# A decoder trunk on one core: compression tiles moved into the recurrence's fill, group norm products spread over projection tiles, three fill chunks per attention step

## The chip, the core and the metric

The kernel runs on one core of a Trainium2 chip. The metric is the device time in microseconds (us) of one execution, the median of several. Below, PE is TensorE, DVE is VectorE, ACT is ScalarE, POOL is GpSimd, SP is the queue that issues most transfers.

## The reference

One decoder layer over 512 tokens of width 1024, all in float32. What matters here:

```python
h = rms_norm(x, norm_pre_mix[l])
proj = h @ w_in[l]
p_rwkv, p_nsa, p_swa, p_gate = _split(proj, (RWKV_COLS, NSA_COLS, SWA_COLS, GATE_COLS))
o_rwkv = rwkv7_time_mix(p_rwkv, ...)   # recurrence over time, then group norm, bonus, output gate g
o_nsa = nsa_mix(p_nsa, ...)            # k_cmp = compress(kc, ..), v_cmp = compress(vc, ..), softmax branches
o_swa = swa_sink_mix(p_swa, ...)       # window of 128 keys with a sink
gates = jax.nn.sigmoid(p_gate)
merged = gates[0] * (o_rwkv @ w_branch[0]) + gates[1] * (o_nsa @ w_branch[1]) + gates[2] * (o_swa @ w_branch[2])
x = x + rms_norm(merged @ w_out, norm_post_mix)
# then a SwiGLU FFN with norms, residual
```

`compress` takes the keys (or values) of NSA in 31 overlapping blocks of 32 tokens, adds a position table `pe`, multiplies the 2048-long blocks by `w1` (2048x256), applies gelu and multiplies by `w2`.

## The kernel before, in words

**Jobs.** Every dense product is a job of the list `JOBS`: one 128-column tile of a weight matrix, 8 chunks of 128 rows (`cmp`: 4 chunks of 128 rows by 256 columns). Order: 14 `rwkv`, 11 `nsa`, 6 `swa`, 5 `gate`, 8 `cmp` (4 for the keys, 4 for the values), 19 more `gate`, then branches, output, FFN. SP loads each tile into one of four buffers `WRAW`. It is split in a high part `WHI` (a rounded copy, by ACT or, for the jobs in `POOL_HI`, by POOL, L568) and a low part `WLO` (always POOL, L564; 128x256 pieces at L599 in attention). There are two split buffers: tile n can be converted when tile n-2 is done, and PE waits at a tile's first chunk for `w_lo`, that is for the whole tile. A chunk is three matmuls (L1481 to L1483; L1489 to L1491 for `cmp`, whose moving operand is the weights and whose stationary operand is the gathered, split input `XHI`, `XLO`). PE accumulates tiles in two banks `DB` by turns (`cmp` in `R[5]`), and DVE evacuates (L999, L1010); a tile starts when the last but one is evacuated. `swa` and `gate` tiles up to a point (`SPILLED`) go through two stage buffers `SQ` to DRAM.

**Fill.** While PE works on the recurrence, the group norm and attention, whose small products depend on DVE and ACT, it calls `fill(point)` between them, which does `FILL[point]` chunks of the next jobs. DVE calls `evacs(point)` at the matching places. The last fill of the gate tiles is `PT_SPLIT`, ahead of the branches.

**Recurrence** (`PT_CP`, four double chunks of time `cp`): in each, five doubling levels `lv`. A level is `pairs(R[0])`, a fill, the wait for `UI` (DVE, L1179), `pairs(R[1])` and `pairs(R[2])`, a fill. Fills of one chunk stand between the levels, larger ones around them (6 at the second point of a `cp`, 4 at its end, 2 at its start).

**Group norm** (`PT_GN`): mean products, variance products, the broadcast of 1/std from 8 rows, the gate product, and four bonus products `gn_bonus(m)`, each of which writes `R[4]` and must wait until DVE has read the one before. Before it DVE gathers `XF` (L1231, 8 operations for keys, 8 for values), copies `XHI` and subtracts to `XLO` (L1234, L1235) for `cmp`. Fills here: 3, 46, 16, 16 (the `cmp` tiles), 8, 16. Then transposes, gelu's second layer, and attention.

**Attention** (`PT_ATT`, 52 steps: for each of four query blocks `i` one compressed step and eight of NSA, keys 128 to 512, then sixteen sliding window steps `swa`): at step n PE does the scores product `qk(n)` (L1764), the fill, the transposes of step n-2 (L1525), the product with the values of step n-3 (L1811). DVE: scores(n), then the reciprocal of step n-1 (L1333). POOL at step n: the weights of step n-1 (`weigh`, L623, L625), then `split_upto(FILLED[PT_ATT + n] + 8)`, which converts pieces of two chunks until 8 chunks past the end of fill n. `FILLED` is the running sum of `FILL`.

```python
            for n in range(NST + 3):
                ...
                if 1 <= n < NST + 1:
                    weigh(n - 1)
                split_upto(int(FILLED[PT_ATT + n]) + 8)
```

Of the kernel before, what the change touches and what calls it, by code (L numbers as in the profile page):

```python
# [24 lines left out]
F32 = mybir.dt.float32  # L25
# [80 lines left out]
for _n in range(11):  # L106
    JOBS.append(("nsa", _n, 0, 8))
SW0 = len(JOBS)
# [3 lines left out]
NGA = 5  # L112
_gates = [("gate", _i, 0, 8) for _i in list(range(3 * GS, 3 * KC)) + list(range(3 * GS))]
JOBS += _gates[:NGA]
CMP0 = len(JOBS)

for _n in range(8):
    JOBS.append(("cmp", _n // 4, _n % 4, 4))
CMP1 = len(JOBS)
NGG = 3  # L120
JOBS += _gates[NGA:3 * (KC - GS)]
# [21 lines left out]
POOL_HI = [n for n in range(NS0, MERGE0) if not CMP0 <= n < CMP1 + NGG]  # L143
# [25 lines left out]
def group_of(n):  # L169

    return sum(not is_cmp(m) for m in range(n))
# [31 lines left out]
PT_ATT = len(FILL); FILL += [2] * (NSA_STEPS + 3)  # L203
# [3 lines left out]
FILL += [2 * (_rest // (2 * (NST - NSA_STEPS)))] * (NST - NSA_STEPS)  # L207
# [30 lines left out]
def build(nc, x, w_in, w_branch, w_out, w_gate, w_up, w_down, w2, a2, g2, ck1, ck2, cv1, cv2, sinks, rel_bias,  # L238
# [49 lines left out]
    T1 = at("T1", 98, [P, 2, 4, C])  # L288
# [21 lines left out]
    XHI = at("XHI", 90, [P, 2, 16, 2 * NCMP], F32R)  # L310
    XLO = at("XLO", 98, [P, 2, 16, 2 * NCMP], F32R)
    XF = at("XF", 52, [P, 16, 2 * NCMP])
# [7 lines left out]
    HG = at("HG", 70, [2 * NCMP, 2, CH])  # L320
# [65 lines left out]
    def split_of(n):  # L386
# [30 lines left out]
    xsplit_ok, cmp_read, hg_u, hg_t, hg_ok, kv_mm, kv_ok = (sem(s) for s in (  # L417
        "xsplit_ok", "cmp_read", "hg_u", "hg_t", "hg_ok", "kv_mm", "kv_ok"))
# [79 lines left out]
    with block:  # L498
# [161 lines left out]
        def _(act):  # L660
# [7 lines left out]
            def hi_part(n):  # L668

                act.wait_ge(w_loaded[n % NRAW], loaded_value(n))  # L670
                if n >= NSPL:
                    act.wait_ge(dense_done, slot_free(n))
                if n in (CMP0, MERGE0):
# [56 lines left out]

            act.wait_ge(cum_ok, 4)
            chunk_exps(0)
            for cp in range(4):
# [9 lines left out]
                for lv in range(1, 6):  # L743
# [7 lines left out]
                    if lv == 4:  # L751
                        act.wait_ge(bkt_T, cp + 1)
                        for c in range(2):
                            act.activation(BKT[:, c, :, :], R[4 + c][:, :].rearrange("p (m n) -> p m n", m=4),
                                           ACT.Copy).then_inc(bkt_ok, 1)
                for c in range(2):
# [14 lines left out]
            hi_part(CMP0)  # L771
            hi_part(CMP0 + 1)
# [4 lines left out]
            act.wait_ge(xsplit_ok, 2)  # L777
            for kv, w in enumerate((ck2, cv2)):
                act.dma_start(CW2[:, kv, :, :], w.rearrange("(h p) d -> p h d", p=P)).then_inc(cw2_in, 16)
            for n in range(CMP0 + 2, CMP0 + 6):  # L780
                hi_part(n)

            def hidden_tanh(kv):
                act.wait_ge(hg_u, kv + 1)
                act.activation(HT[:, kv, :], HT[:, kv, :], ACT.Tanh, scale=0.7978845608028654).then_inc(hg_t, 1)

            act.wait_ge(gn_var, 1)
            act.activation(SSUM[0:NH, :], R[0][0:NH, :], ACT.Sqrt, scale=1.0 / HD, bias=EPSC[0:NH, 1:2]).then_inc(gn_std, 1)
# [14 lines left out]
            act.wait_ge(dense_evac, group_of(NS0 + 10) + 1)  # L803
# [187 lines left out]
        def _(dve):  # L991
# [9 lines left out]
            def evac(n):  # L1001
# [16 lines left out]
                elif kind == "cmp":  # L1018
                    if part == 3:
                        gelu(n, i)  # L1020
                    return
                ins.then_inc(dense_evac, 1)

            def gelu(n, kv):

                dve.wait_ge(dense_done, n + 1)
                dve.tensor_copy(HG[:, kv, :], R[5][0:2 * NCMP, 0:CH]).then_inc(cmp_read, 1)
                dve.wait_ge(cmp_read, kv + 1)
                link(dve.tensor_tensor(HT[:, kv, :], HG[:, kv, :], HG[:, kv, :], ALU.mult))
                link(dve.tensor_scalar(HT[:, kv, :], HT[:, kv, :], 0.044715, 1.0, ALU.mult, ALU.add))  # L1030
                dve.tensor_tensor(HT[:, kv, :], HT[:, kv, :], HG[:, kv, :], ALU.mult).then_inc(hg_u, 1)
                dve.wait_ge(hg_t, kv + 1)
                link(dve.scalar_tensor_tensor(out=HG[:, kv, :], in0=HT[:, kv, :], scalar=1.0, in1=HG[:, kv, :],
                                              op0=ALU.add, op1=ALU.mult))
                dve.tensor_scalar(HG[:, kv, :], HG[:, kv, :], 0.5, None, ALU.mult).then_inc(hg_ok, 1)

            def evacs(point):

                while NS0 + state["evac"] < DONE[point]:
                    n = NS0 + state["evac"]  # L1040
                    if n == CMP0:
                        chain.settle()
# [90 lines left out]

            scaled_bk(0)
            for cp in range(4):
# [39 lines left out]
                for lv in range(1, 6):  # L1175
# [9 lines left out]
                    if lv == 2:  # L1185
# [4 lines left out]
                                          PCS.unsqueeze(2).broadcast_to([P, NH, P]), ALU.mult).then_inc(bkend_ok, 1)  # L1190
                    evacs(pt + 2 + 2 * (lv - 1))
                    evacs(pt + 3 + 2 * (lv - 1))
                for c in range(2):
# [11 lines left out]
                    if c == 0 and cp < 3:  # L1205
# [4 lines left out]
                                      R[2][:, 0:256].rearrange("p (a b) -> p a b", a=4), ALU.add).then_inc(st_ok, 1)  # L1210
                evacs(pt + 16)
# [6 lines left out]

            dve.wait_ge(y_ok, 8)
            for kv in range(2):  # L1220
                dve.wait_ge(dense_evac, group_of(NS0 + 10) + 1)
                pe = PARC[:, PAR["pe"] + 32 * kv:PAR["pe"] + 32 * kv + 32]
                for l in range(2):
                    for g in range(2):
                        p = slice(64 * g, 64 * g + 64)

# [748 lines left out]
```

## Time and profile before

| | us |
|---|---|
| median of 3 runs | 1158.3 (1156.88 to 1160.41) |
| the profiled execution | 1164.61 |
| its span | 1162.7 |
| recurrence, 138.4 to 346.1 | 207.7 |
| group norm and compression, 346.1 to 455.4 | 109.3 |
| attention with its last fills, 455.4 to 659.9 | 204.5 |
| branches, output, FFN, from 659.9 | 502.8 |

PE is busy for 94% of the span. Times of stages are on the profile's clock, from the span's start; "PEclk" in the rows is TensorE's granted clock as a share of full speed.

### The profile page before, as it was taken

The page shows a single profiled execution, that of the slowest core. Times are in us where ns is not written, and L with a number is a line of the kernel's source. Part 1 is how long each engine was busy: PE and PEld are TensorE (multiplying, and loading weights), DVE is VectorE, ACT ScalarE, POOL GpSimd, SP SyncE. Part 2 cuts the span into 40 slices and gives each one's busy share as a digit, 9 for nine tenths or more (in the row PEclk, how much of TensorE's full clock was granted, in tenths as well). Part 3 has the DMA queues.
Part 4 walks back from the last instruction along what each step waited for, and adds up shares of the span by engine and source line. Part 5 has one row for each costly group of instructions (what it writes and reads, how often), then busy time and mean ns, then how long its engine had stood idle before and what let it go on. Part 6 is the DMA issues. An engine that isn't in the chain of part 4 may idle for free.

```text
span 1162.7 us, 19062 instructions
## 1 busy us (share of the span) xinstructions
PE 1087.3 (94%) x7608; PEld 846.5 (73%) x7608; DVE 549.1 (47%) x910; ACT 357.5 (31%) x675; POOL 501.8 (43%) x431
## 2 busy tenths in 40 slices
PE   5998899989996899999998899999999999999996
PEld 3775577777775657666676677788888888888885
DVE  5786744463647162445444367234454454431113
ACT  4222212212110242444444344453322322322222
POOL 1444222221322644665578544743444444444442
PEclk9998899999998989999999999999999999999998
DMA  7343111100233524422111253732333333223231
GB/s 208 91 106 76 46 38 38 39 20 2 80 91 96 186 73 119 136 56 58 34 37 28 72 181 112 234 90 62 100 92 98 100 91 100 83 83 92 86 99 72
DMA packets 166046, 101.83 MB, mean 88 GB/s; under 512 B 21013, under 2 KB 154399, under 8 KB 165976
## 3 DMA queue, kind: packets, MB, share of 16 engines
q1 hardware_dynamic: 162336, 95.96, 28.7%
q10 hardware_dynamic: 3608, 4.88, 1.7%
q8 instruction: 51, 0.84, 0.3%
q14 instruction: 19, 0.16, 0.0%
q0 software_dynamic: 32, 0.00, 0.0%
HBM read 93.19 MB, written 7.63 MB: 87 GB/s over the span
## 4 chain that ended last, share of the span: by engine, by line
PE 80%; DVE 10%; POOL 4%; issue 2%; ACT 2%; DMA 1%; DVEq 0%; ACTq 0%; SPq 0%; POOLq 0%
PE ps L1481 20%; PE ps L1483 18%; PE ps L1482 18%; PE ps L1612 5%; PE ps L1525 3%; PE ps L1764 2%; PE ps L1811 2%; POOL WLO L564 2%; DVE XF L1231 1%; PE ps L1834 1%; PE ps L1836 1%; PE ps L1835 1%; DVE MT L1379 1%; POOL EB L625 1%; DMA PRAW<-in_par 1%
## 5 line engine op out<-in xcount | busy, mean ns | idle before, releaser
L564 POOL TENSOR_TENSOR WLO<-WRAW,WHI 128x1024 fp32r<-128x1024 f32 (+3 forms) x150 | 316.9, 2114 | 346.9 <-ACT WHI L926 197.0
L1481 PE MATMUL ps<-HHI,WHI 128*128 128x512 f32 x776 | 321.7, 415 | 18.1 <-DVE SQ L999 9.6
L1482 PE MATMUL ps<-HLO,WHI 128*128 128x512 f32 x776 | 305.9, 394 | 0.0
L1483 PE MATMUL ps<-HHI,WLO 128*128 128x512 f32 x776 | 305.9, 394 | 0.0
L1481 PEld LDWEIGHTS ps<-HHI,WHI 128*128 128x128 f32 x776 | 147.4, 190 | 75.5 <-issue 29.3
L1483 PEld LDWEIGHTS ps<-HHI,WLO 128*128 128x128 f32 x776 | 147.7, 190 | 32.3
L1482 PEld LDWEIGHTS ps<-HLO,WHI 128*128 128x128 f32 x776 | 147.9, 191 | 27.1 <-issue 1.0
L568 POOL CAST WHI<-WRAW 128x256 fp32r<-128x256 f32 (+1 forms) x83 | 49.0, 590 | 209.5 <-PE ps L1483 209.5
L926 ACT ACTIVATE WHI<-WRAW 128x1024 fp32r<-128x1024 f32 (+2 forms) x72 | 67.5, 937 | 140.0 <-PE ps L1483 140.0
L675 ACT ACTIVATE WHI<-WRAW 128x1024 fp32r<-128x1024 f32 (+1 forms) x55 | 47.8, 870 | 151.1 <-PE ps L1483 134.2
L1432 DVE TENSOR_TENSOR FT<-FT 128x512 f32<-128x512 f32 x22 | 50.9, 2313 | 89.0 <-ACT FT L932 89.0
L825 ACT ACTIVATE EB<-EB,MISC 128x257 f32<-128x257 f32 (+5 forms) x96 | 50.7, 530 | 73.5 <-DVE MISC L1319 59.6
L1481 PE MATMUL ps<-DHI,WHI 128*128 128x512 f32 x176 | 70.0, 398 | 0.2
L1483 PE MATMUL ps<-DHI,WLO 128*128 128x512 f32 x176 | 68.6, 390 | 0.0
L1482 PE MATMUL ps<-DLO,WHI 128*128 128x512 f32 x176 | 68.6, 390 | 0.0
L1449 DVE TENSOR_TENSOR SSUM<-SSUM,SQ 128x512 f32<-128x512 f32 x8 | 14.4, 1794 | 105.1 <-ACT SQ L964 105.1
L623 POOL TENSOR_SCALAR EB<-EB,MISC,GLT 128x128 f32<-128x128 f32 (+3 forms) x64 | 38.3, 607 | 42.1 <-DVE MISC L1333 42.0
L1339 DVE COPY PTB<-ps 128x256 f32<-128x256 f32 (+3 forms) x52 | 23.1, 445 | 60.4 <-PE ps L1525 60.3
L599 POOL TENSOR_TENSOR WLO<-WRAW,WHI 128x256 fp32r<-128x256 f32 x60 | 43.8, 730 | 5.0
L1481 PE MATMUL ps<-OHI,WHI 128*128 128x512 f32 x96 | 38.9, 405 | 5.4 <-POOL WLO L564 5.4
L1319 DVE CUSTOM_DVE_ANT_0 EB<-ps,TB 128x128 f32<-128x128 f32 (+3 forms) x64 | 28.9, 489 | 28.1 <-PE ps L1764 27.8
L934 ACT ACTIVATE DHI<-FT 128x512 f32 (+1 forms) x22 | 13.9, 632 | 88.4 <-DVE FT L1437 88.4
(295 smaller groups left out, 1655.8 us busy)
## 6 DMA issues: line engine op xcount, KB each, us to landing
WRAW<-in_w_in SPq DMA_DIRECT2D x47, 512.0 KB, 4.0
WRAW<-in_w_gate SPq DMA_DIRECT2D x22, 512.0 KB, 3.9
WRAW<-in_w_up SPq DMA_DIRECT2D x22, 512.0 KB, 3.9
WRAW<-in_w_down SPq DMA_DIRECT2D x16, 384.0 KB, 3.5
spilled<-SQ SPq DMA_DIRECT2D x21, 256.0 KB, 2.3
WRAW<-in_w_down SPq DMA_DIRECT2D x16, 320.0 KB, 3.1
WRAW<-in_w_in SPq DMA_DIRECT2D x16, 256.0 KB, 3.5
WRAW<-in_w_branch SPq DMA_DIRECT2D x32, 128.0 KB, 2.8
```

Source lines behind the costliest of these rows:

```text
L564: return pool.tensor_tensor(lo[:, 0:chunks, :], WRAW[:, n % NRAW, 0:chunks, :], hi[:, 0:chunks, :].bitcast(F32), ALU.subtract)
L568: return pool.tensor_copy(WHI[:, n % NSPL, k0:k1, :], WRAW[:, n % NRAW, k0:k1, :])
L599: lo = pool.tensor_tensor(WLO[:, n % NSPL, k:k + 2, :], WRAW[:, n % NRAW, k:k + 2, :], WHI[:, n % NSPL, k:k + 2, :].bitcast(F32), ALU.subt ...
L623: last = pool.tensor_scalar(e, e, rd, GLT[:, i, at0:at0 + 1], ALU.mult, ALU.mult)
L675: act.activation(split_of(n)[0][:, 0:width_of(n), :], WRAW[:, n % NRAW, 0:width_of(n), :], ACT.Copy).then_inc(w_hi, 1)
L825: last = act.activation(EB[:, n % 3, g, 0:w], EB[:, n % 3, g, 0:w], ACT.Exp, scale=-1.0, bias=st[:, g:g + 1], accum_out=st[:, 2 + g:3 + g])
L926: act.activation(WHI[:, n % NSPL, 0:chunks, :], WRAW[:, n % NRAW, 0:chunks, :], ACT.Copy).then_inc(w_hi, 1)
L1432: dve.tensor_tensor(FT[:, b + 1, :], FT[:, b + 1, :], FT[:, b, :], ALU.mult).then_inc(ff_x, 1)
L1481: pe.matmul(dst, WHI[:, s, k, :], hi, start=start, stop=False)
L1482: pe.matmul(dst, WHI[:, s, k, :], lo, start=False, stop=False)
L1483: return pe.matmul(dst, WLO[:, s, k, :], hi, start=False, stop=stop)
L1612: last = pe.matmul(dst[p, j * C:(j + 1) * C], lhsT[p, j, :], rhs(p, j), start=True, stop=True)
```

## The change

- The `cmp` tiles stand in the job order inside the recurrence: the four for the keys after `nsa` 7, the four for the values after `nsa` 10. The keys and values projections (`nsa` 4, 5) come first. `cmp` tiles accumulate in `DB` as the others, and POOL makes their high parts.
- The gather becomes four DVE operations of 64x496 for each product (`compress_in`), one per level 1 to 4 of `cp` 0 and of `cp` 2, placed after the level's own DVE work. ACT makes `XHI` after the levels (`x_high`), DVE subtracts at the end of the `cp` (`compress_low`). `XHI`, `XLO`, `XF` are held once, and `XLO` lies on `XF`.
- The group norm has 11 fills. Gelu is done once for both products (62x512).
- Attention has 3 chunks per step instead of 2, and the last step ahead of `PT_SPLIT` 6 instead of 12. The fill chunks of all points together are 360 before and after.
- Fill chunks up to the first attention step: 232 before (200 of full width, 32 `cmp`), 184 after (152 and 32).

```diff
-for _n in range(11):
+for _n in (4, 5, 0, 1, 2, 3, 6, 7):
     JOBS.append(("nsa", _n, 0, 8))
+CMP0 = len(JOBS)
+for _n in range(4):
+    JOBS.append(("cmp", 0, _n, 4))
+for _n in (8, 9, 10):
+    JOBS.append(("nsa", _n, 0, 8))
+NSA_LAST = len(JOBS) - 1
+for _n in range(4):
+    JOBS.append(("cmp", 1, _n, 4))
...
-POOL_HI = [n for n in range(NS0, MERGE0) if not CMP0 <= n < CMP1 + NGG]
+POOL_HI = list(range(NS0, MERGE0))
...
-PT_GN = len(FILL); FILL += [3, _left - 3, 16, 16, 8, 8 * (NGG - 1)]
+PT_GN = len(FILL); FILL += [3, 6, 6, 6, 4, 4, 8, 8, 4, 4, 4]
...
-PT_ATT = len(FILL); FILL += [2] * (NSA_STEPS + 3)
+PT_ATT = len(FILL); FILL += [3] * (NSA_STEPS + 3)
...
-FILL += [2 * (_rest // (2 * (NST - NSA_STEPS)))] * (NST - NSA_STEPS)
+FILL += [_rest // (NST - NSA_STEPS)] * (NST - NSA_STEPS)
...
+            def compress_in(kv, step):
+
+                l, g = step // 2, step % 2
+                if step == 0:
+                    dve.wait_ge(dense_evac, 16)
+                    if kv:
+                        dve.wait_ge(dense_done, CMP0 + 4)
...
+                dve.tensor_tensor(XF[64 * l:64 * l + 64, :, g * NCMP:(g + 1) * NCMP], v,
+                                  pe[p, :, l:l + 1].broadcast_to([64, 16, NCMP]), ALU.add).then_inc(xf_ok, 1)
...
+                    if cp % 2 == 0 and lv < 5:
+                        compress_in(cp // 2, lv - 1)
                     evacs(pt + 2 + 2 * (lv - 1))
...
+                if cp % 2 == 0:
+                    compress_low(cp // 2)
                 evacs(pt + 16)
...
             gn_bonus(0)
-            fill(PT_GN + 1)
-            gn_bonus(1)
             fill(PT_GN + 2)
...
             last.then_inc(gn_var, 1)
+            gn_bonus(1)
+            fill(PT_GN + 3)
             gn_bonus(2)
-            fill(PT_GN + 3)
+            fill(PT_GN + 4)
             gn_bonus(3)
+            fill(PT_GN + 5)
```

After the broadcast of 1/std stands a fill of 8, after the gate product another of 8, and one of 4 each after the transposes to token order, after gelu's transposes and after the second layer's products.

## Rows read from the trace of the kernel before

**Rows 1.** Waits of PE: releaser, us in total, times, longest.
```profile
PE ps L1481 <- DVE SQ L999: 9.6, 1, 9.6
PE ps L1489 <- POOL WLO L564: 7.4, 5, 2.2
PE ps L1481 <- POOL WLO L599: 6.8, 9, 1.6
```
**Rows 2.** Windows by stage: length, busy time (instructions), then PEclk, DMA share, GB/s.
```profile
346.10:455.40 109.30, 90.40 (x396) 64.57 (x394) 50.14 (x70) 25.23 (x29) 48.15 (x26) 0.89 0.47 132
455.40:659.90 204.50, 197.61 (x1351) 140.18 (x1350) 90.83 (x351) 85.40 (x266) 133.40 (x235) 0.99 0.21 59
```
**Rows 3.** The gather's line: durations in ns (lowest, median, highest), first and last start.
```profile
L1231 DVE TENSOR_TENSOR XF<-NQ,PARC x16: 559/574/2649, 345.6 to 360.7; 64x248 f32<-64x248 f32 x16
```
**Rows 4.** PE, timeline of the group norm stretch: products, dense and compression chunks.
```profile
346.12 3.59 PE L1695 MATMUL ps<-KK,CONP 128*128 128x512 f32 x8
349.55 1.02 PE L1701 MATMUL ps<-CUM,CONP 128*128 128x512 f32 x2
...
392.58 0.39 PE L1481 MATMUL ps<-HHI,WHI 128*128 128x512 f32 x1
393.26 1.02 PE L1701 MATMUL ps<-CUM,CONP 128*128 128x512 f32 x2
...
394.47 0.28 PE L1489 MATMUL ps<-WHI,XHI 128*62 128x256 f32 x1
394.82 0.28 PE L1489 MATMUL ps<-WHI,XHI 128*62 128x256 f32 x1
```
**Rows 5.** PE, timeline: a fill of one chunk between two products of a recurrence level.
```profile
155.14 0.50 PE L1481 MATMUL ps<-HHI,WHI 128*128 128x512 f32 x1
156.04 1.15 PE L1612 MATMUL ps<-UI,XS 64*64 64x64 f32 x32
```
**Rows 6.** DVE, timeline: `UI` of level 2, and DVE's idle time before it.
```profile
160.14 0.69 DVE L1179 TENSOR_TENSOR UI<-ps,MASK 128x512 f32<-128x512 f32 x1 [1.80 <-PE ps L1612]
```
**Rows 7.** POOL, timeline: one tile converted whole, in level 1.
```profile
156.24 1.19 POOL L568 CAST WHI<-WRAW 128x1024 fp32r<-128x1024 f32 x1 [7.50 <-PE ps L1483]
157.51 2.37 POOL L564 TENSOR_TENSOR WLO<-WRAW,WHI 128x1024 fp32r<-128x1024 f32 x1
```
**Rows 8.** PE, timeline: an NSA step of 512 keys.
```profile
560.94 1.13 PE L1764 MATMUL ps<-NQ 64*128 64x512 f32 x4
562.00 0.50 PE L1481 MATMUL ps<-HHI,WHI 128*128 128x512 f32 x1
...
565.48 1.13 PE L1764 MATMUL ps<-NQ 64*128 64x512 f32 x4
```
**Rows 9.** POOL, timeline: the low part of that step's piece.
```profile
565.55 0.72 POOL L599 TENSOR_TENSOR WLO<-WRAW,WHI 128x256 fp32r<-128x256 f32 x1
```
**Rows 10.** PE and POOL, timeline: an NSA step of 128 keys and its piece.
```profile
465.87 0.49 PE L1764 MATMUL ps<-NQ 64*128 64x128 f32 x4
...
468.41 0.73 POOL L599 TENSOR_TENSOR WLO<-WRAW,WHI 128x256 fp32r<-128x256 f32 x1
```
**Rows 11.** PE and POOL, timeline: a sliding window step that waits, and its piece.
```profile
624.49 0.70 PE L1764 MATMUL ps<-SWQ 64*128 64x256 f32 x4
626.11 0.50 PE L1481 MATMUL ps<-HHI,WHI 128*128 128x512 f32 x1 [0.92 <-POOL WLO L599]
...
628.57 0.72 POOL L599 TENSOR_TENSOR WLO<-WRAW,WHI 128x256 fp32r<-128x256 f32 x1
```
**Rows 12.** PE, timeline: two longer waits outside the group norm.
```profile
196.80 0.38 PE L1603 MATMUL ps<-AR,BK 64*128 64x128 f32 x2 [2.64 <-DVE AR L1144]
...
665.83 0.50 PE L1481 MATMUL ps<-OHI,WHI 128*128 128x512 f32 x1 [3.07 <-POOL WLO L564]
```
**Rows 13.** Windows behind these two waits, columns as in rows 2.
```profile
196.80:200.20 3.40, 3.40 (x38) 3.06 (x39) 1.24 (x3) 1.13 (x2) 0.00 (x0) 1.00 0.78 154
667.00:670.00 3.00, 3.00 (x9) 2.32 (x8) 0.00 (x0) 0.00 (x0) 0.03 (x1) 0.50 0.64 167
```

More of the change, by code:

```diff
@@ L111 @@
 GS = 3
-NGA = 5
 _gates = [("gate", _i, 0, 8) for _i in list(range(3 * GS, 3 * KC)) + list(range(3 * GS))]
[L114 to L121, printed above, removed]
+JOBS += _gates[:3 * (KC - GS)]
 GC0 = len(JOBS)
@@ L169, in group_of @@
 def group_of(n):
-    return sum(not is_cmp(m) for m in range(n))
+    return sum(not is_cmp(m) or JOBS[m][2] == 3 for m in range(n))
 def width_of(n):
@@ L309, in build @@
     GATES = at("GATES", 90, [P, 15, T])
-    XHI = at("XHI", 90, [P, 2, 16, 2 * NCMP], F32R)
-    XLO = at("XLO", 98, [P, 2, 16, 2 * NCMP], F32R)
-    XF = at("XF", 52, [P, 16, 2 * NCMP])
+    XHI = at("XHI", 92, [P, 16, 2 * NCMP], F32R)
+    XF = at("XF", 96, [P, 16, 2 * NCMP])
+    XLO = at("XLO", 96, [P, 16, 2 * NCMP], F32R)
+    GNS = at("GNS", 56, [NH, T])
     small = Region(Z + int(118.5 * KB))
@@ L729, in chunk_exps, with x_high @@
                 act.activation(E2[:, :, :], CUM[:, :, at0], ACT.Exp, scale=-1.0).then_inc(exp_ok, 1)
+            def x_high(kv):
+                act.wait_ge(xf_ok, 4 * kv + 4)
+                act.activation(XHI[:, :, :], XF[:, :, :], ACT.Copy).then_inc(xhi_ok, 1)
             act.wait_ge(cum_ok, 4)
@@ L1217, in _, with gn_bonus @@
             evacs(PT_GN)
+            def gn_bonus(m):
+                dve.wait_ge(gn_bmm, m + 1)
+                dve.tensor_tensor(AA[:, m, :], R[4][:, :], RW[:, 8 + m, :], ALU.mult).then_inc(gn_b, 1)
             dve.wait_ge(y_ok, 8)
[L1220 to L1225, printed above, removed]
[L1227 to L1237 removed]
             for m in range(4):
@@ L1472, in rhs @@
                     kv, c = i, 4 * part + k
-                    return XHI[:, kv, c, :], XLO[:, kv, c, :]
+                    return XHI[:, c, :], XLO[:, c, :]
                 if kind == "branch":
@@ L1500, in steps @@
                         pe.wait_ge(w_lo, n + 1)
-                        if g >= 2 and kind != "cmp":
+                        if g >= 2 and part == 0:
                             pe.wait_ge(dense_evac, g - 1)
@@ L1504, in steps @@
                             pe.wait_ge(xsplit_ok, i + 1)
-                            if i == 1 and part == 0:
-                                pe.wait_ge(cmp_read, 1)
                         if kind == "branch":
@@ L1512, in steps @@
                     if kind == "cmp":
-                        last = cmp_product(n, k, hi, lo, part == 0 and k == 0, part == 3 and k == 3)
+                        last = cmp_product(DB[g % 2], n, k, hi, lo, part == 0 and k == 0, part == 3 and k == 3)
                     else:
@@ L1716, in _ @@
             for m in range(4):
-                pe.matmul(R[m][:, :], SELT[1][:, m, :], SSUM[0:NH, :], start=True, stop=True).then_inc(gn_bc, 1)
+                pe.matmul(R[m][:, :], SELT[1][:, m, :], GNS[:, :], start=True, stop=True).then_inc(gn_bc, 1)
+            fill(PT_GN + 6)
             pe.wait_ge(g2_in, 16)
@@ L1721, in _ @@
                 pe.matmul(R[m][:, :], WA[:, m * P:(m + 1) * P], RW[:, 13, :], start=True, stop=True).then_inc(gn_bc, 1)
[L1722 to L1723 removed]
+            fill(PT_GN + 7)
             pe.wait_ge(gn_ok, 4)
@@ L1733, in _ @@
             last.then_inc(vtok_T, 1)
+            fill(PT_GN + 8)
             pe.wait_ge(cw2_in, 32)
-            pe.wait_ge(hg_ok, 2)
+            pe.wait_ge(hg_ok, 1)
             for i in range(4):
@@ L1738, in _ @@
             last.then_inc(kv_mm, 1)
-            pe.wait_ge(hg_ok, 3)
+            fill(PT_GN + 9)
+            pe.wait_ge(hg_ok, 2)
             for g in range(2):
@@ L1747, in _ @@
             last.then_inc(kv_mm, 1)
+            fill(PT_GN + 10)
             pe.wait_ge(kv_ok, 1)
```

114 lines of the change are left out of this document (50 added, 64 removed).

## The prediction

> **What bounds the kernel now.** The page's first part comes first: PE is busy for 94% of the span, so the time is PE's work at full clock, plus its waits, plus what it loses at the low clock. Then the waits of PE [rows 1]: 9.6 us once for an evacuation, 7.4 us for the low parts of compression tiles, both in the group norm stretch, and 6.8 us in nine waits for POOL's pieces, all in attention. Then the windows by stage [rows 2]: the stretch of 109.3 us has 18.9 us of idle PE and a mean granted clock of 0.89; the 204.5 us of attention have 6.9 us idle and 0.99. So the loss sits in the first, and attention is bound by PE. The change moves work between stages and adds or removes no matmul of weight, so each stage is summed for itself, and the difference of the sums is the forecast. From 659.9 us on nothing changes: the chain there starts at the last product of attention, and the fills behind it (8 gate chunks, 4 of a branch) stay.
>
> **Group norm stretch.** The 9.6 us wait comes from 16 gather operations [rows 3] with their copies, ahead of an evacuation in DVE's order. They leave, with it. What PE still does here: a product of 512 columns takes two records, 8 records take 349.55 - 346.12 = 3.43 us, so 0.86 each [rows 4]. Four means, four variances, four broadcasts, four gate products and four bonus products: 20 x 0.86 = 17.2. Transposes, gelu's second layer and the first compressed scores take the last 6.2 us of the stretch less waits of 1.9: 4.3. A dense chunk costs 393.26 - 392.58 = 0.68 [rows 4]. A fill of one chunk between small products takes 156.04 - 155.14 = 0.90 [rows 5], so each fill adds some 0.2 for the change of kind. The ten fills after the first have 54 chunks: 54 x 0.68 + 10 x 0.2 = 38.7. Sum 60.2. Waits: the closest point is the third bonus product, which needs DVE's second, behind the variance, the square root on ACT (0.7) and DVE's reciprocal of 8x512 (3.3). PE has one bonus and six chunks there, 5.1 us, against about 5.0. The chain of gate product, DVE's two operations per tile, sigmoid with table load is about 2 us shorter than the gate product and the eight chunks behind it. I add 1.0. 61.2 instead of 109.3: **-48.1**.
>
> **Recurrence.** 32 dense chunks leave its fills and 32 compression chunks come, 394.82 - 394.47 = 0.35 each [rows 4]: 32 x (0.35 - 0.68) = -10.6. Not all is won. Six of the places stand ahead of `UI`, and there the slot of 0.90 is already about what DVE needs (0.1 to start, 0.69, 0.1 to release) [rows 5, 6]: six times 0.33, and 0.3 at two places that wait for DVE's copies, come back as waits, 2.3. POOL now makes high and low part of each compression tile, 1.19 + 2.37 and the release, about 3.7 us [rows 7], and may start only when the tile two before is done. Where compression tiles stand densely PE runs short: after `nsa` 10 in the last `cp`, four chunks cover 1.4 of 3.7 us, wait 2.3; at the turn to the third `cp` the same, of which 1.3 remain since a wait for DVE ends there. DVE's gather: one operation of 64x496, twice the old form's elements, about 1.1 us from the median 0.574 [rows 3]. DVE idles 1.80 us ahead of `UI` in level 2 [rows 6], about as much ahead of level 3 and more later, so it hides, in eight places. If that cover were gone each would cost its 1.1. But POOL converts a tile in level 1, until 159.9 [rows 7], and the gather there would begin at 157.7; the maximum of its row is 2.65 against the median 0.57 [rows 3], so I take it as held up until POOL ends: 1.0 late. ACT's copy and DVE's `compress_low` (1.2) fall in gaps of 3 us. Sum -10.6 + 2.3 + 2.3 + 1.3 + 1.0 = -3.7.
>
> The Trainium skill ("SBUF — State Buffer", Who interferes with whom) says that a VectorE instruction with two inputs in SBUF contends with a GpSimd instruction that reads SBUF, and that the one issued second blocks until the first ends. By it every gather that meets a low part is held up for the rest of its 2.37 us, in the order of DVE's list; the maximum in rows 3 agrees.
>
> **Attention.** 48 more chunks of 0.68: +32.6. At its start the granted clock is low now for 3 us after waits that a fill will cover: -1.7. Then the waits. PE may start a tile only when its last piece is converted, and POOL's step n converts to eight chunks past the end of fill n. With two chunks per step a tile starts at the start of a fill, and step s-1's pieces suffice. With three, tiles start in turn at the second chunk of a fill, at the first, and at the third. In that third case the pieces of step s-1 end at 8 chunks past its own end, two short of the tile's end, so PE, having done two chunks of fill s, needs the first piece of POOL's step s, which stands behind `weigh`. Times from the scores product of the same step: at 512 keys the piece ends 566.27 - 560.94 = 5.33 [rows 8, 9]; PE gets there at 1.06 + 0.90 + 0.68 = 2.64 [rows 4, 5, 8]; wait 2.7. At 128 keys 469.14 - 465.87 = 3.27 [rows 10] against 0.42 + 1.58: wait 1.3. In the window steps 629.29 - 624.49 = 4.80 [rows 11] against 0.63 + 1.58: wait 2.6. Tiles start so in steps 2, 10, 18, 26, 34, 42 and 50 (fill positions 192, 216, and every 24th to 336): 1.3 + 2.1 + 2.4 + 2.3 + 2.7 + 2.6 + 2.6 = 16.0, those between put between the ends by their key count and the longer chain of a compressed step. The same reading gives the waits of now: a window step is 3.24, its fill starts 0.63 on, the piece of the step before ends at 4.80, wait 0.93; the trace has 0.92 [rows 11]. The other two kinds of tile start have more room than now (at 512 keys a step becomes 4.54 + 0.68, so PE comes at 6.3 for a piece that ends at 5.3); only the window steps keep 1.5 in sum. New waits 17.5 for the 6.8 of now: +10.7.
>
> **Clock.** A wait of 3.07 us was followed by a granted clock of 0.50, so 1.2 GHz, for over 3 us, one of 2.64 by none [rows 12, 13]. Such a stretch costs half its length, 1.7. Of six waits of over 2 us in attention and two in the recurrence I take half: +5.1 and +1.7. Bounds 0 and +13.6.
>
> **Sum.** Group norm -48.1; recurrence -3.7 + 1.7 = -2.0; attention 32.6 - 1.7 + 10.7 + 5.1 = +46.7. Together -3.4. The profiled execution had a span of 1162.7 and a time of 1164.6, which is 6.3 over the median of 1158.3; I take the difference as it is: **1154.9**, call it 1155. Most of the gain in the group norm is not a gain: 32.6 of it is work moved, and half of the rest goes to the waits at every third tile. The bound of what the measurement can tell is 0.3%, 3.5 us, so this stands on the edge.
>
> **Rivals.** *No wait at the third chunk.* If POOL's piece were there, as it would be if `weigh` ended before PE has done two chunks, the new waits and their clock fall away, and attention is 32.6 - 1.7 with the old waits: +30.9. Sum -48.1 - 2.0 + 30.9 = -19.2, 1139. Against it: 5.33 to 2.64 is far apart [rows 8, 9]. For it: I read the order of pieces from the code, and no trace here has such a wait.
>
> *A wait at every tile.* The other two kinds of tile start wait too, 14 more, because POOL's two-piece steps end one piece (1.15) later than I think and push the next `weigh`. 14 x 1.15 = 16, so 1171, slower than before. It decides from where PE's room of about 0.9 at 512 keys is used up. For it: POOL is the busiest in the window steps and already the releaser of all nine waits [rows 1].
>
> *The gather on DVE's path.* Held up by POOL each time at levels 1 and 2, an operation is 3.2 long, 1.4 over its gap [rows 3, 6]: 4 x 1.4 + 0.7 at the turn of the `cp`, less the 1.0 counted: +5.3, 1160. That is the skill's rule at its full size; against it, a tile ends only about every 20 us in the recurrence, so most gathers meet no conversion [rows 7].
>
> *The group norm stays a chain.* With 57 chunks instead of 105 to cover the same DVE and ACT steps, PE waits 10 instead of 1: 1164. Against it the sums above, with a term of room at each place.
>
> **Chances.** Forecast 0.50, its own range 1149 to 1161 (the clock's bounds, a few us for the unknown waits). No wait at the third chunk 0.18. Wait at every tile 0.12. Gather 0.15. Chain 0.05. Faster means below 1154.8: half of the forecast less a little for its upper tail, 0.25, all of the first rival and a little of the third, 0.45. Slower, above 1161.8: the second, the fourth, a third of the gather and a tail, 0.23. Same 0.32. The range must take in 1139 with a margin and leaves the wait at every tile out: 1137 to 1164.
>
> **What would show it.** In the profile after: PE's wait on `SQ` (L999) gone and the group norm stretch near 61 us; XHI and XLO waits on POOL twice in the recurrence, near 2 us; in attention seven waits of 1.3 to 2.7 us for POOL's low part, each in the middle of a fill, after two chunks, in every eighth step; low clock behind some of them; attention near 251 us. `UI` later by 1 us in level 1 of the first `cp` only. I am wrong if attention shows no wait inside a fill, or one at each tile, or if the group norm stretch is over 66 us.

## The result

The changed kernel takes **1174.9 us** (median of four runs, 1173.64 to 1175.45) beside 1159.4 us for the kernel before, run on the same chip. The ratio is 1.0123, 95% interval 1.0094 to 1.0151: slower by 1.2%. The forecast was 1155.0 with a range of 1137 to 1164, so the time lies outside the range, and on the other side of no change.

First the waits of PE in the changed kernel's profile, to be held against [rows 1]: releaser, us in total, times, longest.

```profile
PE ps L1482 <- POOL WLO L598: 16.7, 10, 2.7
...
PE ps L1482 <- POOL WLO L563: 6.9, 9, 3.1
PE ps L1490 <- POOL WLO L563: 4.8, 2, 2.6
PE ps L1611 <- DVE XC L1182: 5.3, 4, 2.7
...
PE ps L1611 <- DVE UI L1189: 3.4, 6, 1.2
PE ps L1602 <- DVE AR L1154: 2.6, 1, 2.6
PE ps L1656 <- DVE ST L1221: 2.5, 1, 2.5
```

The wait of 9.6 us for an evacuation is gone. In its place stand 16.7 us for POOL's pieces in attention (L598), where before there were 6.8.

Then the windows of the same three stages, cut at the same products: the recurrence, the group norm stretch, attention. Columns as in [rows 2].

```profile
138.28:352.58 214.30, 195.13 (x3211) 159.58 (x3212) 114.91 (x170) 41.10 (x76) 62.49 (x35) 0.93 0.16 44
352.58:412.09 59.51, 59.51 (x251) 39.98 (x249) 28.40 (x41) 13.93 (x17) 24.67 (x17) 1.00 0.51 129
412.09:669.46 257.37, 240.57 (x1494) 171.94 (x1493) 94.81 (x357) 86.20 (x266) 159.71 (x284) 0.96 0.24 68
```

The recurrence of the kernel before, which [rows 2] doesn't hold:

```profile
138.43:346.12 207.69, 198.02 (x3211) 158.85 (x3212) 100.94 (x163) 39.27 (x74) 48.24 (x27) 0.98 0.16 40
```

So the group norm stretch fell by 49.8 us, the recurrence grew by 6.6 and attention by 52.9. Sum +9.7; the rest of the span is 0.7 shorter, and the profiled executions differ by +9.0 (1173.6 to 1164.6). Read the columns together. Length less PE's busy time is idle PE: in attention 257.37 - 240.57 = 16.8 us. Where PE runs the same products, a longer busy time points to a lower clock, and the PEclk column says how much: 0.93 in the recurrence for 0.98, 0.96 in attention for 0.99.

Now one of the seven waits, the third chunk of the fill in step 18, on PE and then on POOL (start, duration, operation, idle time and releaser in brackets).

```profile
482.70 0.40 PE L1484 MATMUL ps<-HHI,WLO 128*128 128x512 f32 x1
485.61 0.80 PE L1482 MATMUL ps<-HHI,WHI 128*128 128x512 f32 x1 [2.51 <-POOL WLO L598]
486.20 0.63 PE L1483 MATMUL ps<-HLO,WHI 128*128 128x512 f32 x1
```

```profile
483.32 1.09 POOL L622 TENSOR_SCALAR EB<-EB,MISC,GLT 128x256 f32<-128x256 f32 x2 [2.86 <-DVE MISC L1334]
484.35 0.40 POOL L567 CAST WHI<-WRAW 128x256 fp32r<-128x256 f32 x1
484.83 0.72 POOL L598 TENSOR_TENSOR WLO<-WRAW,WHI 128x256 fp32r<-128x256 f32 x1
```

This is the predicted mechanism: POOL sat idle for 2.86 us ahead of `weigh` (L622), waiting for DVE's statistics, and the piece that PE needs stands behind it in POOL's list. In the other six the piece stands behind the weighting too. How long POOL idled ahead of the weighting differs, from 2.55 us in the fifth to 0.25 in the sixth, where POOL's own work fills the step. What comes behind the wait is the part that the forecast took at half: the same product takes 0.63 there and 0.39 at full clock. Four windows of 3 us, started behind a wait of 2.51, 2.67 and 2.58 in attention and one of 2.54 in the recurrence:

```profile
485.70:488.70 3.00, 3.00 (x13) 2.27 (x15) 0.55 (x2) 0.38 (x1) 0.93 (x2) 0.50 0.02 5
571.40:574.40 3.00, 3.00 (x11) 2.50 (x11) 0.00 (x0) 0.00 (x0) 0.99 (x2) 0.53 0.00 0
646.20:649.20 3.00, 3.00 (x15) 1.82 (x12) 1.69 (x7) 0.63 (x4) 0.06 (x1) 0.50 0.28 82
240.00:243.00 3.00, 3.00 (x30) 2.22 (x32) 0.62 (x2) 0.38 (x1) 0.00 (x0) 0.50 0.32 97
```

PE is busy all through, at the lower of its two levels (1.2 GHz) but for a last bit in the second window.

### The profile page after: what moved, and what is told of

Same layout as the page of the kernel before. It is cut to its first block, busy times and chain, and to the rows that moved or that the text cites. A ratio compares the mean times of both kernels' runs of the same rounds, so it can differ in the third digit from the quotient of the medians.

```text
span 1171.8 us, 19083 instructions
## 1 busy us (share of the span) xinstructions
PE 1096.0 (94%) x7608; PEld 854.0 (73%) x7608; DVE 545.3 (47%) x895; ACT 348.9 (30%) x665; POOL 518.8 (44%) x478
## 4 chain that ended last, share of the span: by engine, by line
PE 82%; DVE 8%; POOL 5%; issue 2%; ACT 2%; DMA 1%; ACTq 0%; DVEq 0%; POOLq 0%
PE ps L1482 20%; PE ps L1484 18%; PE ps L1483 18%; PE ps L1611 5%; PE ps L1524 4%; PE ps L1768 3%; PE ps L1815 2%; POOL WLO L563 2%; PE ps L1838 1%; PE ps L1839 1%; PE ps L1840 1%; POOL EB L624 1%; POOL WLO L598 1%; DVE MT L1380 1%; PE ps L1602 1%
## 5 line engine op out<-in xcount | busy, mean ns | idle before, releaser
L563 POOL TENSOR_TENSOR WLO<-WRAW,WHI 128x1024 fp32r<-128x1024 f32 (+3 forms) x144 | 303.3, 2107 | 319.2 <-ACT WHI L916 197.0
L1482 PE MATMUL ps<-HHI,WHI 128*128 128x512 f32 x776 | 324.0, 417 | 18.3 <-POOL WLO L598 16.7
L1484 PEld LDWEIGHTS ps<-HHI,WLO 128*128 128x128 f32 x776 | 147.8, 190 | 32.6
L567 POOL CAST WHI<-WRAW 128x256 fp32r<-128x256 f32 (+1 forms) x112 | 63.4, 566 | 208.9 <-PE ps L1484 174.9
L598 POOL TENSOR_TENSOR WLO<-WRAW,WHI 128x256 fp32r<-128x256 f32 x84 | 61.3, 729 | 7.0
L622 POOL TENSOR_SCALAR EB<-EB,MISC,GLT 128x128 f32<-128x128 f32 (+3 forms) x64 | 38.3, 609 | 57.8 <-DVE MISC L1334 57.6
L674 ACT ACTIVATE WHI<-WRAW 128x512 fp32r<-128x512 f32 (+1 forms) x44 | 36.2, 824 | 79.8 <-PE ps L1484 74.9
L823 ACT ACTIVATE PTB<-ps 128x256 f32<-128x256 f32 (+3 forms) x52 | 20.8, 400 | 76.6 <-PE ps L1524 76.3
L749 ACT ACTIVATE XC<-ps 128x512 f32<-128x512 f32 x16 | 9.6, 597 | 111.5 <-PE ps L1611 111.5
```

Of the source, the lines that this page charges most:

```text
L563: return pool.tensor_tensor(lo[:, 0:chunks, :], WRAW[:, n % NRAW, 0:chunks, :], hi[:, 0:chunks, :].bitcast(F32), ALU.subtract)
L567: return pool.tensor_copy(WHI[:, n % NSPL, k0:k1, :], WRAW[:, n % NRAW, k0:k1, :])
L598: lo = pool.tensor_tensor(WLO[:, n % NSPL, k:k + 2, :], WRAW[:, n % NRAW, k:k + 2, :], WHI[:, n % NSPL, k:k + 2, :].bitcast(F32), ALU.subt ...
L622: last = pool.tensor_scalar(e, e, rd, GLT[:, i, at0:at0 + 1], ALU.mult, ALU.mult)
L1482: pe.matmul(dst, WHI[:, s, k, :], hi, start=start, stop=False)
L1484: return pe.matmul(dst, WLO[:, s, k, :], hi, start=False, stop=stop)
```

## The experiments

### Attention: what the third-chunk waits cost

Three ways to have the piece there in time, each on the changed kernel. **POOL's pieces two chunks further ahead:**

```diff
-                split_upto(int(FILLED[PT_ATT + n]) + 8)
+                split_upto(int(FILLED[PT_ATT + n]) + 10)
```

> POOL's pieces in an attention step go two chunks further ahead of the fill (10 instead of 8), so the low part of a tile's first chunk is there before a fill that crosses a tile's end reaches it. Theory A (the attention's excess is the seven mid-fill waits of 15.5 us together and the six low-clock stretches that stand behind them, some 10 us): the seven waits go, one or two of the low-clock stretches remain, and the time is 18 to 24 us under that of the changed kernel, 1151 to 1157 us. Rival B (the waits only stand where POOL's or VectorE's work would end the step anyway, so another wait takes their place): within 4 us of the changed kernel, 1171 to 1178 us.

Measured: 1145.6 us, ratio to the kernel before 0.9866 (0.9826 to 0.9907). That is 29 us under the changed kernel, more than the 18 to 24 that theory A said. PE has no wait left in attention.

**A tile only at the start of a fill:**

```diff
-PT_ATT = len(FILL); FILL += [3] * (NSA_STEPS + 3)
+PT_ATT = len(FILL); FILL += [3, 3, 2] * ((NSA_STEPS + 3) // 3)
```

> The fill of the attention's 512-key steps goes 3, 3, 2 chunks instead of 3 each, so that no fill crosses a tile's end: a tile starts only at the start of a step's fill. The chunks that this gives up (a third of a chunk per step) go to the last, short steps. Theory A (the excess of the attention is waits at a tile's start in the middle of a fill): the seven waits go, 1153 to 1160 us, a little less gained than by going further ahead, since the last steps get longer fills of 4 chunks and may wait there. Rival B (the cost is in the number of chunks and POOL's work, not in where a tile starts): 1171 to 1178 us.

Measured: 1152.8 us, ratio 0.9935 (0.9915 to 0.9955), at the lower edge of theory A's range. Thirteen shorter waits, none over 0.93 us, take 7.8 us; PEclk is 1.00 over the stage.

```profile
PE ps L1482 <- POOL WLO L598: 7.8, 13, 0.9
```

```profile
411.19:648.61 237.42, 229.53 (x1494) 166.27 (x1493) 95.05 (x357) 85.94 (x266) 160.09 (x284) 1.00 0.26 74
```

**POOL's pieces ahead of its own weighting:**

```diff
+                split_upto(int(FILLED[PT_ATT + n]) + 8)
                 if 1 <= n < NST + 1:
                     weigh(n - 1)
-                split_upto(int(FILLED[PT_ATT + n]) + 8)
```

> In each attention step POOL makes the pieces of the next tile's low part before its own softmax weighting instead of behind it; how far ahead it goes is left. Theory A: the pieces come some 2 us earlier in a step, which takes most of each mid-fill wait of 1.2 to 2.7 us, so the time falls by 10 to 20 us against the changed kernel, to 1155 to 1165 us. Rival B: the softmax weighting, now late by a piece of some 1 to 2 us in each step, ends what the next products wait for, and the time stays within 4 us of the changed kernel or rises above 1180 us.

Measured: 1145.6 us, ratio 0.9867 (0.9825 to 0.9910), again more gain than theory A's 10 to 20 us. The windows of its three stages:

```profile
138.05:349.52 211.47, 192.35 (x3210) 157.82 (x3211) 114.61 (x170) 41.14 (x76) 62.51 (x35) 0.94 0.17 44
349.52:412.28 62.76, 62.76 (x252) 41.61 (x250) 28.40 (x41) 13.92 (x17) 24.69 (x17) 0.95 0.49 124
412.28:640.85 228.57, 228.57 (x1494) 166.23 (x1493) 94.87 (x357) 86.16 (x266) 160.75 (x284) 1.00 0.27 77
```

Attention is now all work: busy 228.57 of 228.57, clock 1.00. The same 1494 products took 240.57 busy in the changed kernel. So its excess of 28.8 us splits into 16.8 of idle PE and 12.0 of longer busy time. A granted clock of 0.96 over 257.37 us is 20.6 us at the lower level, which costs half of that, 10.3; the remaining 1.7 no row assigns. The longest of these stretches stands behind the wait of 2.20:

```profile
526.40:533.20 6.80, 6.80 (x42) 5.69 (x41) 2.70 (x7) 0.49 (x1) 0.00 (x0) 0.50 0.41 118
```

Rival B is out in all three: POOL is as busy as in the changed kernel (160.75 for 159.71 us in this one), and no other wait takes the place. The late weighting that B feared costs nothing that PE shows.

**The clock alone.** The changed kernel again with its waits' places kept, but PE busy in part of each (the line for `w_lo` is moved down here from ahead of the wait for the bank):

```diff
+                        if attention and step == 2:
+                            for _ in range(6):
+                                pe.matmul(DB[g % 2][:, :], HHI[:, 0, 0:P], HHI[:, 0, :], start=True, stop=True)
                         pe.wait_ge(w_lo, n + 1)
```

> The changed kernel (1174.9 us) with one addition: at the seven tiles of the attention whose first chunk is the third of a fill, PE multiplies six times 128x512 into the tile's own bank (which the tile's first product then overwrites) before it waits for the low part. The six products take some 1.4 us, so they fit into six of the seven waits of 1.24 to 2.67 us and add about 0.2 us at the first; nothing else comes earlier or later. Theory A (the waits of 15.5 us are only half of the cost, and the low-clock stretches behind them the rest): the waits shrink to 6 us or so, the low clock of the attention goes for the most part, and the time falls by 7 to 10 us to 1165 to 1168 us. Rival B (the low clock there has another cause, or costs little because POOL sets the pace): 1173 to 1176 us.

Measured: 1166.6 us, ratio 1.0044 (1.0027 to 1.0062), 8.3 under the changed kernel although PE does 42 products more. PE at the same tile as above, then the window of attention:

```profile
481.50 1.53 PE L1505 MATMUL ps<-HHI 128*128 128x512 f32 x6
484.18 0.50 PE L1482 MATMUL ps<-HHI,WHI 128*128 128x512 f32 x1 [1.15 <-POOL WLO L598]
```

```profile
412.16:661.45 249.29, 240.88 (x1537) 173.30 (x1535) 94.79 (x357) 86.14 (x266) 159.68 (x284) 1.00 0.25 70
```

The idle time fell from 16.8 to 8.4 us, which by itself wins nothing, as the six products fill it. The granted clock rose from 0.96 to 1.00, and that is the gain: the recurrence and the group norm stretch are the changed kernel's to the tenth (214.3 and 59.5 us). Theory A's time came as put (1165 to 1168), and the clock's share is shown apart from the waits.

### The recurrence: why it grew

**ACT makes two high parts**, those of the fourth keys tile (`CMP0 + 3`) and the second values tile (`CMP0 + 8`, which the expectation calls the first), on the changed kernel:

```diff
-POOL_HI = list(range(NS0, MERGE0))
+ACT_HI = (CMP0 + 3, CMP0 + 8)
+POOL_HI = [n for n in range(NS0, MERGE0) if n not in ACT_HI]
...
+                if cp == 1:
+                    hi_part(ACT_HI[0])
```

> The high parts of two compression tiles that run in the recurrence (the fourth of keys, the first of those after three dense tiles) are made by ACT instead of POOL, so POOL has 2 of its conversions less there. Theory C (POOL's conversions in the recurrence make PE wait for the low part of the compression tiles and hold up VectorE's operations, and low-clock stretches follow): the waits of 2.2 and 2.6 us go, with one or two low-clock stretches of 1.7 us cost each, and the time falls by 3 to 8 us, to 1167 to 1172 us. Rival D (recurrence is longer by its own added work, and another wait takes over): within 2 us of the changed kernel, 1173 to 1177 us.

Measured: 1174.9 us, the changed kernel's own median. The two waits are 2.22 and 2.50 us. ACT's copy starts when POOL's would have, since both wait for the tile two before to be done, and takes as long (1.06 for 1.04). So moving the high part off POOL doesn't shorten the wait; what is left as its cause is the length of the conversion behind the free slot. That part of theory C falls.

The runs from here on stand on the version with POOL's pieces first (1145.6 us), so that attention is out of the way. The next three, and the one on the group norm stretch, ran on another chip than the others (the kernel before took 1161.4 us there, and 1160.3 beside the version with the pieces first), so a difference of 1 or 2 us between them and the 1145.6 says nothing. **Chunks dealt out otherwise:**

```diff
-    PT_CP.append(len(FILL)); FILL += [5 if _cp == 0 else 2, 6] + [1, 1] * 5 + [1, 1, 1, 1, 4]
+    PT_CP.append(len(FILL)); FILL += [5 if _cp == 0 else 2, 4 if _cp == 3 else 6, 2 if _cp == 3 else 1, 1] + [1, 1] * 4
+    FILL += [1, 1, 1, 2, 3] if _cp == 1 else [1, 1, 1, 1, 5 if _cp == 2 else 4]
```

> On the version with POOL's pieces first in an attention step (1145.6 us), the fill of the recurrence is dealt out otherwise with the same sum: one chunk more before the second chunk pair ends (so the slot of the second keys tile comes free some 4 us earlier), one more at the end of the third pair, and 4 and 2 chunks instead of 6 and 1 at the start of the fourth. Theory C (PE runs through a compression tile in 1.4 us and waits for POOL's conversion of 3.6 us of the one after next, and low-clock stretches follow): the waits of 2.25 and 2.57 us go and some of the low clock with them, 1137 to 1142 us. Rival D (the conversion is as late wherever the chunks stand, or the low clock comes all the same from the recurrence's small products): 1144 to 1147 us.

Measured: 1144.3 us (1142.6 to 1146.5). Both waits for the low part went, and others came in their places. Waits of PE on its timeline:

```profile
248.96 1.27 PE L1603 MATMUL ps<-AR,BK 64*128 64x128 f32 x18 [1.46 <-DVE AR L1155]
...
305.54 1.15 PE L1612 MATMUL ps<-MASK,AM 64*64 64x64 f32 x32 [1.77 <-DVE AM L1170]
309.58 0.69 PE L1612 MATMUL ps<-XC,AM 64*64 64x64 f32 x8 [2.90 <-DVE XC L1183]
```

POOL's low part, now earlier, lies on DVE's first operations of the fourth pair. That is rival D's result by another way: the recurrence stays at 211.8 us, for 211.5.

**BK scaled later.** In the changed kernel and in this version DVE scales the next pair's `BK` while POOL converts. DVE, then POOL, in the version with the pieces first:

```profile
233.40 0.67 DVE L1118 TENSOR_TENSOR BK<-AA,E 128x512 f32<-128x512 f32 x1
234.00 2.83 DVE L1119 TENSOR_TENSOR BK<-RW,E 128x512 f32<-128x512 f32 x1
236.75 0.41 DVE L1221 TENSOR_TENSOR ST<-ST,ps 128x256 f32<-128x256 f32 x1
```

```profile
233.59 2.69 POOL L563 TENSOR_TENSOR WLO<-WRAW,WHI 128x1024 fp32r<-128x1024 f32 x1
```

The second scaling begins 0.41 us after the low part and ends 0.55 us after its end; the one ahead of it took 0.67. PE waits 2.53 us for the state behind it.

```diff
-                    if c == 0 and cp < 3:
+                    if c == (cp == 1) and cp < 3:
                         scaled_bk(cp + 1)
```

> On the version with the pieces first (1145.6 us), VectorE scales the next pair's BK in the second half of the second chunk pair's end instead of the first, so that its two operations no longer lie on POOL's low part of 2.7 us (one of them took 2.83 us instead of 0.67) ahead of the state's update. Theory C2 (POOL's conversions, which the compression tiles bring into the recurrence, hold up VectorE's operations of the chain): the wait of 2.53 us for the state goes, and 0 to 2 low-clock stretches, 1140 to 1144 us. Rival D2 (the scaling is as late where it now stands, and the wait moves to the next pair's first products): 1144 to 1148 us.

Measured: 1142.2 us (1141.8 to 1144.1), ratio 0.9838 (0.9811 to 0.9866; that of the version under it is 0.9867, and the two intervals overlap). The wait is gone and no other takes its place, as theory C2 has it. In the profiled execution the recurrence gains little by it:

```profile
137.74:348.56 210.82, 194.17 (x3211) 158.76 (x3212) 112.82 (x170) 41.10 (x76) 62.63 (x35) 0.94 0.17 45
```

Idle PE fell from 19.1 to 16.7 us, and busy time rose from 192.35 to 194.17. That execution is the slowest of the five. The mechanism is shown; the size of the gain, 3.4 us by the medians, is not settled.

**Both edits together:**

> Both edits of the two kernels before on the version with the pieces first (1145.6 us). If the waits of the recurrence each cost what they take and the low clock behind them as well, 1133 to 1139 us; if only the waits count, 1138 to 1140 us; if other waits take their place, 1144 to 1147 us.

Measured: 1142.4 us (1140.5 to 1143.3), above both cases in which the waits add up and no better than the second edit alone. The two waits for DVE in the fourth pair, which the first edit brings, stay (1.77 and 2.90). **The second edit with one chunk moved forward in the second pair only** (`FILL += [1, 1, 2, 1, 3] if _cp == 1`):

> The version with POOL's pieces first and BK scaled later (1142.2 us), with one chunk moved forward in the second pair's last steps, so that the second keys tile's slot is free some 5 us earlier, and nothing changed in the fourth pair. If the wait of 2.27 us for the fourth keys tile goes and nothing takes its place: 1138 to 1141 us; if VectorE's AR ends the same gap (0.9 us of it stood there in the combined version): 1140 to 1142 us; no gain: 1142 to 1143 us.

Measured: 1142.8 us (1142.3 to 1144.1): a wait of 1.36 for the low part and 0.90 for `AR` stand for the one of 2.27. No gain, the time of its third case by the mechanism of its second.

**Without the conversions:**

```diff
-                    hi_part(n, 0, width_of(n)).then_inc(w_hi, 1)
+                    hi_part(n, 0, 1 if is_cmp(n) else width_of(n)).then_inc(w_hi, 1)
                 pool.wait_ge(w_hi, n + 1)
-                lo_part(n, width_of(n)).then_inc(w_lo, 1)
+                lo_part(n, 1 if is_cmp(n) else width_of(n)).then_inc(w_lo, 1)
```

> On the version with POOL's pieces first (1145.6 us) POOL converts only a sixteenth of each of the eight compression tiles (128x128 instead of 128x1024), so that part of the computation is left out; PE's products and all waits stay. Theory C (what makes the recurrence longer than before the change is POOL's conversions of compression tiles, which PE waits for and which hold up VectorE): both waits for the low part, the state's 2.53 us and the excess of the other VectorE waits go, and the recurrence falls from 211.5 us to 200 to 204 us, the time to 1134 to 1138 us. Rival E (the loss is the low clock that follows from the compression chunks being small products, too little work in a level): the waits go but the low clock stays or spreads, recurrence 206 to 211 us, 1140 to 1146 us.

This kernel leaves out fifteen sixteenths of the conversion of the compression tiles. Measured: 1131.6 us (1129.5 to 1134.6), 13.9 under the version with the pieces first and more than theory C's 7 to 11. The recurrence:

```profile
139.18:336.41 197.23, 185.63 (x3211) 152.11 (x3212) 106.51 (x170) 41.11 (x76) 40.32 (x35) 0.98 0.18 47
```

It fell by 14.2 us, 7.5 of it idle PE (11.6 for 19.1) and 6.7 busy time at a clock of 0.98 for 0.94. All products, the gather and `compress_low` are still there. So the compression chunks as small products don't lower the clock (rival E is out); POOL's conversions cost the whole 14 us, by PE's waits for them, by DVE's operations that they hold up, and by the clock behind both. And 207.69 - 197.23 = 10.5, where the forecast counted 10.6 for the lighter chunks. That is a net, though: PE's busy time is 12.4 less than before the change (an estimated 1.5 of it clock, as the lower level covers 6.6 us of the stage for 9.6), and its idle time 1.9 more; and POOL has less to do here than before the change (40.32 us for 48.24), as four dense tiles left the stage too.

### The group norm stretch: is it cover?

```diff
-PT_GN = len(FILL); FILL += [3, 6, 6, 6, 4, 4, 8, 8, 4, 4, 4]
+PT_GN = len(FILL); FILL += [3, 29, 0, 0, 0, 0, 16, 0, 0, 0, 9]
```

> On the version with the pieces first (1145.6 us), the 57 chunks of the group norm stretch stay, but stand at three places instead of between all of its steps: 3 and 29 ahead of the bonus products, 16 ahead of the gate's product, 9 at the end. Theory G (the stretch fell from 109 to 60 us because dense chunks cover a chain of VectorE and ACT whose steps are still as long): PE waits for the variance, the reciprocal of 3.3 us and the transposed values, 8 to 16 us of waits and one to four low-clock stretches, so 1155 to 1168 us. Rival H (the chain was short once the gather was out of it, and the order of the chunks matters little): 1145 to 1149 us.

Measured: 1165.0 us (1162.3 to 1166.5), 19.5 over the version with the pieces first, and within theory G's range. Its waits in the stretch, and the window:

```profile
PE ps L1729 <- ACT GL L794: 4.7, 1, 4.7
...
PE ps L1700 <- DVE AA L1235: 4.6, 2, 3.7
```

```profile
350.30:430.62 80.32, 70.52 (x251) 45.66 (x249) 26.54 (x41) 13.93 (x17) 24.65 (x17) 0.83 0.35 89
```

The same products and chunks take 80.3 us instead of 62.8: 9.8 of waits and 7.8 of clock, which is 17.6 of the 19.5. The steps of DVE and ACT that PE waits for here are in the other version too; the spread chunks cover them.

## Why the prediction was wrong

Point by point, in the order of its sum.

**Group norm, -48.1: right.** 59.5 us for 61.2, no wait of PE in it for the 1.0 that was added. The tenth is luck: with the same instructions there, the stretch took 62.8 in the version with the pieces first. That the spread chunks now cover the chain is shown by the run with the chunks pulled together. How the 49.8 divide between that, the gather that left and the clock, no run shows. One sentence of the sum's comment is wrong: "32.6 of it is work moved". The 32.6 is what attention got; the stretch gave 16 dense and 32 compression chunks, 16 x 0.68 + 32 x 0.35 = 22.1, and the recurrence the other 10.6.

**Recurrence, work -10.6: borne out as a net** by the run without conversions (10.5), though the forecast wanted 2.3 of it back as waits. **Its waits, +6.9: too small by 2.6.** Idle PE went from 207.69 - 198.02 = 9.7 to 214.30 - 195.13 = 19.2, +9.5. The two low-part waits came (2.23 and 2.57 for 1.3 and 2.3; the first stands where the kernel before waited 1.28 for `AR`, so it adds 1.0). The gather was held up for most of a low part once in eight, in level 1 of the first pair; another of the eight took 1.65:

```profile
L1135 DVE TENSOR_TENSOR XF<-NQ,PARC x8: 989/1004/3041, 157.4 to 280.9; 64x496 f32<-64x496 f32 x8
```

The wait for `UI` behind it was 0.97, as forecast. What the step missed is that the gather is not the only DVE operation to meet a low part. The scaling of `BK` took 2.83 (wait for the state 2.54, which is nearly all of the 2.6), the end scaling of `BK` 2.78 (wait for `UI` 1.23), two `AM` 4.08 together (wait for `XC` 2.69). The kernel before had shown it at that last place, where an operation of its own took 2.83 beside POOL's conversion and the wait for `XC` was 2.10; I read neither row:

```profile
252.47 2.83 DVE L1170 TENSOR_TENSOR XS<-AM,MASK 128x512 f32<-128x512 f32 x1
```

```profile
252.08 2.67 POOL L564 TENSOR_TENSOR WLO<-WRAW,WHI 128x1024 fp32r<-128x1024 f32 x1
```

The Trainium skill ("SBUF — State Buffer", Who interferes with whom) says that such a DVE instruction blocks until the GpSimd one that was issued first ends. These rows agree: `XS` begins 0.39 us after POOL's low part and ends 0.55 behind its end, as the scaling of `BK` above. I applied the rule to the operations that the change adds and not to the ones that were there, though it is the change that puts conversions beside them.

**Attention, 32.6 of work: right to the tenth.** 204.5 - 6.9 idle + 32.6 less the 1.7 is 228.5; the version without waits measures 228.57. **The new waits: right.** Seven, in the steps named, 1.24, 1.74, 2.51, 2.20, 2.67, 2.57 and 2.58 = 15.5 for 16.0, and 16.7 in all for 17.5.

**The clock, +5.1 and +1.7: this step failed.** "Of six waits of over 2 us in attention and two in the recurrence I take half" was priced at 6.8 with an upper bound of 13.6. In attention PE's busy time grew by 12.0 (the version without waits has the same products, and the run with busy waits gives most of it back), 6.9 more than taken; 10.3 of it by the clock column. In the recurrence PE's busy time fell by 2.9 where the work fell by 10.6: 7.7 of clock for 1.7. Together 19.7, or 18.0 by the clock column's 10.3, above the bound itself either way. The bound was wrong because it counted one stretch of 1.7 us for each of eight waits over 2 us. The wait of 2.57 at 609.0 had none behind it; but in the trace a low clock also followed the wait of 1.74, one of 6.8 us the wait of 2.20, and the recurrence's waits for DVE (`ST`, `XC`, `AR`), which the step didn't count at all, brought theirs. The trace of before had such rows: behind its wait of 2.10 for `XC` at 256.05 stands a low clock.

```profile
257.20:260.60 3.40, 3.40 (x40) 2.66 (x41) 2.49 (x4) 0.00 (x0) 0.00 (x0) 0.50 0.02 5
```

The forecast priced the step from two rows and read half from one yes and one no. Windows of the changed kernel, 3 us each: behind the wait of 1.74, then behind the 2.57 at 308.59 and its two successors:

```profile
450.00:453.00 3.00, 3.00 (x14) 1.83 (x15) 1.26 (x5) 0.28 (x1) 0.90 (x2) 0.72 0.05 18
...
308.60:311.60 3.00, 2.79 (x35) 2.27 (x35) 2.08 (x3) 0.00 (x0) 2.92 (x2) 0.50 0.73 153
312.30:315.30 3.00, 3.00 (x40) 2.53 (x41) 2.04 (x4) 0.00 (x0) 0.44 (x1) 0.50 0.50 103
315.30:318.30 3.00, 3.00 (x62) 3.00 (x62) 1.48 (x3) 0.60 (x1) 0.00 (x0) 0.52 0.37 77
```

**The reference point: failed too.** I subtracted 6.3 us because the profiled execution of before lay that far above the median of its three runs, and let the changed kernel inherit it. Its own profiled execution lies 1.3 below its median. The record shows what the 6.3 was: over 42 later executions the kernel before took 1156.6 to 1165.5 us, the fastest at a mean clock of 0.980 and the slowest at 0.973, with medians of 1160.3 to 1161.5. The profiled execution had 0.975. So the distance goes with the clock that the one execution was granted, and the median of three was itself low. Misses in the profile 12.4 (busy time beyond the work +6.9 and +6.0, waits in the recurrence +2.6, group norm -1.7, attention's waits -0.7, the rest of the span -0.7), reference point 6.3 + 1.3: together the 20.0 by which 1154.9 falls short of 1174.9.

Of the rivals, "no wait at the third chunk" has its version: 1145.6 us measured for 1139 put. With POOL's pieces first the changed kernel is 1.3% faster than the kernel before, and 1.6% with `BK` scaled later. What made it a loss was where POOL's piece stands in a list, not the work moved. How much of the 1.3% is the change's own is open: the kernel before has 6.8 us of waits for POOL's pieces in attention too, and no run puts its pieces first.

Left open: when a wait is followed by a low clock. Attention is the same in the changed kernel and in the run where ACT makes two high parts; behind the third wait, 2.51 in the one and 2.53 in the other, the clock was 0.50 in the one and this in the other:

```profile
484.90:487.90 3.00, 3.00 (x20) 1.94 (x21) 1.15 (x3) 0.38 (x1) 1.01 (x2) 1.00 0.02 5
```

The same wait of 2.64 us for `AR` was followed by a clock of 1.00 before [rows 12, 13] and by 0.50 in the changed kernel from 199.0 on, with the same products around it:

```profile
199.00:202.00 3.00, 3.00 (x18) 2.49 (x15) 1.54 (x4) 0.00 (x0) 0.00 (x0) 0.50 0.42 148
```

Nor is it settled why the group norm stretch has 1.00 in the changed kernel and 0.95, 3.2 us longer, in the version with the pieces first, without a wait in either. The recurrence, with the same instructions and 19.1 to 19.3 us of idle PE in all, took 214.3 us in the changed kernel and with the busy waits, 211.5 with the pieces first and 212.0 with tiles at the start of a fill. So 3 us of a stage's time come and go with the clock from one profiled kernel to the next, and of the 7.7 above only some 5 are in every trace. That is still more than the 1.7 of the forecast.

## What to carry to other kernels

A wait of 2 us on TensorE costs nearly twice its length when a low-clock stretch follows (in attention 16.8 us of idle time came with 12.0 us of longer busy time), so price the two together, count every wait of 1.7 us and more, whatever releases it, and don't take one stretch for each as the upper bound. Look for a cheap reorder of the releasing engine's list before giving up a move of work. When a change puts GpSimd conversions beside a chain on VectorE, list every two-input VectorE operation of that chain, old ones too. Compare a sum made from one profiled execution with that execution alone; its distance from the median doesn't carry over, since here it went with the clock granted in that execution.

## What the hardware showed that was not expected

Filling a wait with products whose results are thrown away paid: 42 of them, some 9.7 us at the 0.23 that products start apart, made the program 8.3 us shorter, as the granted clock in attention went from 0.96 to 1.00. Thirteen waits of up to 0.93 us (7.8 us in sum) left it at 1.00, while seven of 1.24 to 2.67 (15.5) brought it to 0.96.
